# Softmax attention steps put in another order, bf16 decay rows and a new order of side work in a two-block transformer kernel on one Trainium2 core

## The chip, the cores and the metric

The kernel runs on one core of one Trainium2 chip. A core has four engines that compute: TensorE (PE, matrix products and transposes; its weight loads are shown apart as PEld), VectorE (DVE), ScalarE (ACT) and GpSimd (POOL), and SyncE (SP), whose queue issues nearly all weight loads here. Each engine works through its own queue in order, so an instruction that waits holds up all that stand behind it. The metric is the device time of one execution in microseconds (us); less is better.

## The reference

A 256 x 1024 activation `x` goes through a first block of two layers and a second block of two layers, all in fp32.

```python
# first block; layer 0 is even, layer 1 odd
y = even_mixer(rms(x))      # layer 0: 8 "fox" heads with a decay + 8 "nsa" heads (selected, window, compressed)
y = diff_mixer(rms(x))      # layer 1: 8 pairs of heads, a1 - lam * a2
x = x + rms(y); x = x + rms(memory_cross_attention(rms(x), rms(mem))); x = x + rms(swiglu(rms(x)))
# second block, each layer
x = x + 0.5 * swiglu(rms(x))
z = rms(x) @ w_in
mixed = sum(sigmoid(gate_i) * (y_i @ w_i))  # y: neighborhood attention, gated linear attention, latent attention
x = x + mixed @ w_out; x = x + 0.5 * swiglu(rms(x))
# fox attention
c = cumsum(log_sigmoid(f + bias)); s = q @ k.T / 8 + (c_q - c_k); p = softmax(masked s); o = p @ v
```

The softmax drops what is the same for all keys of a row, so of `c_q - c_k` only `-c_k` is added.

## The kernel before

All activations stay on chip. The 256 rows are two row tiles (`TT = 2`). A product with a weight matrix (`gemm_steps`) runs over *units* of weights of up to 2048 columns per partition: SP loads a unit into `raw`, ACT rounds it to `w_hi` (L449), DVE subtracts to get `w_lo` (L454, written over `raw`), and PE makes three products for each block of 128 weight rows (L593 to L595). There are six raw slots and three `w_hi` slots (`RAW_SLOTS`, `HI_SLOTS`). `part` emits the rounding and the subtraction, in one piece or in four.

Python generators are *fillers*: `fill(n)` emits n steps of work from them, a step of a weight product being six PE instructions (two blocks of rows, one row tile). A unit takes four steps. Outside attention `take` has every free unit prepared whole; within attention (`turn["gentle"]`) units are prepared in four pieces by `trickle`.

`attention(groups, ...)` handles two heads at a time (a group). In the order of the loop before: `trickle(2)`, `scores(i)` (PE: mask L805, q k L811), `turned(i-1)` (PE: transposes of the probabilities, L908), `maxed(i)` (DVE: row maximum, L842 or, with a bias, L835 and L838), `copied(i-1)` (transposes to `pT`, one half on ACT L921, the other on DVE L927), `exped(i)` (ACT, L867), `fill(a)`, `normed(i)` (DVE, L886 and L893), `summed(i-1)` (PE: value products L952, L958, L965), `fill(b)`. `probs` has one buffer. The plan gives (a, b) for each group.

There are these attention stages, in the profile's time: the even mixer (70 to 269 us; fox groups 0 to 3, then 12 nsa groups), memory attention (313 to 329 and 720 to 737 us, two groups, no filler), the odd mixer (578 to 672 us, 8 groups), neighborhood attention (1190 to 1274 and 1925 to 2007 us, 4 groups) and latent attention (1419 to 1450 and 2152 to 2184 us, 2 groups). The even mixer's fillers (`side`) are the nsa projections, then in this order the rotations of queries and keys with the gate's sigmoid (`sparse_keys`, L1343 to L1381, L1641, L1631), the memory keys and values of layer 0 (`memory_steps(0)`: transposes L532 with h_hi L568 and h_lo L584, then products), transposes, `compress` (L1680 to L1749) and `memory_steps(1)`. `rotate` shares its work between DVE and POOL and has one instruction for each row tile.

The decay of the fox heads is added by fp32 matmuls between the q k ones: a row of ones out of `ident` (8 rows) times `c_neg` (8 x 256), one for each head and row tile (L811, named `hT,const`).

## Time and profile before

| what | value |
|---|---|
| time, median of 3 runs | 2414.78 us (2404.65 to 2421.23) |
| the profiled execution, its time | 2420.43 us |
| its span, first to last instruction | 2418.8 us |
| PE busy | 2151.5 us (89%) |
| DVE busy | 1267.2 us (52%) |
| ACT busy | 1024.6 us (42%) |
| POOL busy | 165.1 us (7%) |
| TensorE clock granted, mean | 0.929 |

The span lies 1.6 us under the execution's own time, and that time 5.7 us over the median. The granted clock is the mean of two levels, 1.0 (2.4 GHz) and 0.5 (1.2 GHz).

### The profile page before, as it was taken

How to read it: one execution, taken by the hardware profiler on the slowest of the kernel's cores; microseconds unless marked ns; L12 is line 12 of the kernel's file. 1: busy time of each engine (PE TensorE's matmuls, PEld its weight loads, DVE VectorE, ACT ScalarE, POOL GpSimd, SP SyncE). 2: the span in 40 equal slices, each digit the busy share in tenths (PEclk: the TensorE clock that was granted, in tenths of full speed). 3: DMA queues.
4: the chain of work that ended last, by engine and by line, in shares of the span. 5: the costliest groups of instructions: out<-in, count | busy, mean ns of one | idle time of the engine just before them, and what ended most of it. 6: DMA issues, size and time to landing. Idle time of an engine off the chain costs nothing.

```text
span 2418.8 us, 26665 instructions
## 1 busy us (share of the span) xinstructions
PE 2151.5 (89%) x9943; PEld 1742.9 (72%) x9956; DVE 1267.2 (52%) x1767; ACT 1024.6 (42%) x1507; POOL 165.1 (7%) x200
## 2 busy tenths in 40 slices
PE   6968879999778999999978979999999978879998
PEld 5746568877566887887757757887887766757887
DVE  4435554555655445545455556545555546565454
ACT  4234444444444434444335435444444436345442
POOL 0010000000100000000202030000000202030000
PEclk8876779999888999999888989999999998989999
DMA  8212225554123554655533324655555433224553
GB/s 263 78 54 88 79 95 181 187 181 157 44 87 125 183 189 156 192 191 166 164 96 109 129 72 157 191 190 164 187 190 191 151 117 97 100 96 155 186 184 102
DMA packets 247751, 346.14 MB, mean 143 GB/s; under 512 B 28292, under 2 KB 177608, under 8 KB 247624
## 3 DMA queue, kind: packets, MB, share of 16 engines
q1 hardware_dynamic: 245816, 340.37, 44.0%
q10 hardware_dynamic: 1264, 2.79, 0.3%
q8 instruction: 81, 1.33, 0.2%
q0 software_dynamic: 544, 1.29, 0.2%
q14 instruction: 46, 0.38, 0.0%
HBM read 343.35 MB, written 2.33 MB: 143 GB/s over the span
## 4 chain that ended last, share of the span: by engine, by line
PE 76%; issue 8%; DVE 7%; ACT 4%; POOL 3%; ACTq 0%; DVEq 0%; POOLq 0%
PE bank L593 23%; PE bank L595 22%; PE bank L594 22%; DVE w_lo L454 2%; PE bank L811 2%; ACT w_hi L449 1%; PE bank L1088 1%; PE bank L958 1%; ACT h_hi L568 1%; PE bank L532 1%; DVE jobstat L842 1%; POOL o_buf L2080 1%; ACT probs L867 1%; DVE x L1249 1%; PE bank L952 1%
## 5 line engine op out<-in xcount | busy, mean ns | idle before, releaser
L454 DVE TENSOR_TENSOR w_lo<-raw,w_hi 128x2048 fp32r<-128x2048 f32 (+6 forms) x453 | 736.0, 1645 | 504.3 <-ACT w_hi L449 503.5
L593 PE MATMUL bank<-w_hi,h_hi 128*128 128x512 f32 (+4 forms) x1936 | 786.1, 406 | 135.4 <-DVE w_lo L454 85.6
L594 PE MATMUL bank<-w_lo,h_hi 128*128 128x512 f32 (+4 forms) x1936 | 767.1, 396 | 0.0
L595 PE MATMUL bank<-w_hi,h_lo 128*128 128x512 f32 (+4 forms) x1936 | 766.5, 396 | 0.0
L449 ACT CAST w_hi<-raw 128x2048 fp32r<-128x2048 f32 (+6 forms) x453 | 613.3, 1380 | 277.5 <-PE bank L595 265.7
L593 PEld LDWEIGHTS bank<-w_hi,h_hi 128*128 128x128 f32 x1936 | 383.7, 198 | 226.6 <-issue 69.9
L595 PEld LDWEIGHTS bank<-w_hi,h_lo 128*128 128x128 f32 x1936 | 382.4, 198 | 75.2
L594 PEld LDWEIGHTS bank<-w_lo,h_hi 128*128 128x128 f32 x1936 | 384.7, 199 | 68.6
L593 PE MATMUL bank<-w_hi,ff_hi 128*128 128x512 f32 x528 | 206.1, 390 | 0.0
L595 PE MATMUL bank<-w_hi,ff_lo 128*128 128x512 f32 x528 | 205.5, 389 | 0.0
L594 PE MATMUL bank<-w_lo,ff_hi 128*128 128x512 f32 x528 | 205.5, 389 | 0.0
L1067 ACT ACTIVATE ff_silu<-bank,rs 128x256 f32<-128x256 f32 x132 | 55.6, 472 | 200.9 <-PE bank L595 200.9
L1099 ACT CAST ff_hi<-bank 128x512 fp32r<-128x512 f32 x66 | 38.7, 587 | 235.8 <-PE bank L1088 235.8
L593 PEld LDWEIGHTS bank<-w_hi,ff_hi 128*128 128x128 f32 x528 | 99.1, 188 | 21.0 <-DVE ff_lo L1104 0.3
L1104 DVE TENSOR_TENSOR ff_lo<-bank,ff_hi 128x512 fp32r<-128x512 f32 x66 | 45.6, 691 | 131.0 <-ACT ff_hi L1099 131.0
L595 PEld LDWEIGHTS bank<-w_hi,ff_lo 128*128 128x128 f32 x528 | 99.1, 188 | 20.7
L594 PEld LDWEIGHTS bank<-w_lo,ff_hi 128*128 128x128 f32 x528 | 99.2, 188 | 20.3
L1076 DVE SCALAR_TENSOR_TENSOR ff_hid<-bank,rs,ff_silu 128x256 f32<-128x256 f32 x132 | 57.8, 479 | 86.3 <-ACT ff_silu L1067 86.3
L698 POOL TENSOR_TENSOR rs<-rs,const 128x2 f32<-128x2 f32 (+2 forms) x27 | 31.9, 1183 | 1041.4 <-DVE rs L693 1041.4
L568 ACT ACTIVATE h_hi<-bank,cols 128x256 fp32r<-128x256 f32 x128 | 49.9, 482 | 78.5 <-PE bank L532 48.7
L584 DVE SCALAR_TENSOR_TENSOR h_lo<-bank,cols,h_hi 128x256 fp32r<-128x256 f32 x128 | 52.3, 477 | 41.6 <-ACT h_hi L568 41.6
L811 PE MATMUL bank<-kT,qT 64*128 64x256 f32 (+2 forms) x320 | 61.1, 404 | 8.5 <-DVE kT L550 5.1
(248 smaller groups left out, 1665.0 us busy)
## 6 DMA issues: line engine op xcount, KB each, us to landing
raw<-in_ffn_w SPq DMA_DIRECT2D x176, 512.0 KB, 4.7
raw<-in_w_in SPq DMA_DIRECT2D x52, 1024.0 KB, 5.1
raw<-in_ffn_w SPq DMA_DIRECT2D x44, 1024.0 KB, 4.9
raw<-in_ffn_wg SPq DMA_DIRECT2D x44, 512.0 KB, 4.0
raw<-in_ffn_wu SPq DMA_DIRECT2D x44, 512.0 KB, 5.0
raw<-in_ffn_wd SPq DMA_DIRECT2D x22, 1024.0 KB, 4.8
raw<-in_od_w_in SPq DMA_DIRECT2D x12, 1024.0 KB, 5.1
raw<-in_w_out SPq DMA_DIRECT2D x8, 1024.0 KB, 5.1
```

The costliest lines, as they stand in the source:

```text
L449: act.copy(hi[:, cs], raw_[:, cs]).then_inc(*act_did.up())
L454: dve.tensor_tensor(lo_[:, cs], raw_[:, cs], hi[:, cs].bitcast(F32), ALU.subtract).then_inc(*dve_did.up())
L568: act.activation(dst(b0 + b, 1), ps[:, b:b + 1, :], ACT.Copy, scale=scale(b0 + b)).then_inc(*act_did.up())
L584: dve.scalar_tensor_tensor(dst_lo(b0 + b, 1), ps[:, b:b + 1, :], scale(b0 + b), dst(b0 + b, 1).bitcast(F32), ALU.mult, ALU.subtract).then_ ...
L593: pe.matmul(out, x_hi, u.hi[:, k, cols_], start=start, stop=False)
L594: pe.matmul(out, x_hi, u.lo[:, k, cols_], start=False, stop=False)
L595: return pe.matmul(out, x_lo, u.hi[:, k, cols_], start=False, stop=stop)
L811: mm = pe.matmul(view(i, j)[:, tt, 0:g["n"][tt]], l, r, start=(m == 0 and not masked), stop=(m == len(pairs) - 1), skip_group_check=True)
L1067: act.activation(ff_silu[:, c % 2, tt, :], bank.t[:, 0:FF_CHUNK], ACT.Silu, scale=r(tt)).then_inc(*act_did.up())
L1076: dve.scalar_tensor_tensor(ff_hid[:, c % 2, tt, :], bank.t[:, FF_CHUNK:2 * FF_CHUNK], r(tt), ff_silu[:, c % 2, tt, :], ALU.mult, ALU.mult) ...
L1099: act.copy(ff_hi[:, c % 2, :, :], ps).then_inc(*act_did.up())
L1104: dve.tensor_tensor(ff_lo[:, c % 2, :, :], ps, ff_hi[:, c % 2, :, :].bitcast(F32), ALU.subtract).then_inc(*dve_did.up())
```

## The change

- Attention loop: the order is now `turned(i-1)`, `copied(i-1)`, `fill(a)`, then `begin(i+1)` (`scores`, `maxed`, `exped` of the next group), `normed(i)`, `fill(b)`, `summed(i-1)`. `probs` has two buffers; `pT` lies in a spare half of `gain` or in `o_buf`. The 1/8 is put on q while it is copied out of its transposes, so that the separate scaling of the row maxima goes. `normed` takes the reciprocals of both heads in one instruction.
- Weights: in attention every filler step also calls `trickle` once; the subtraction of a piece is emitted after the rounding of the next; a unit is not begun until one step after its `w_hi` slot was last used (`LAG`).
- Fox decay: `-c` is split into three bf16 parts in 72 rows (`c3`), and one bf16 matmul of 512 columns for each head adds it.
- Even layer: the memory transposes and products are cut into four and put among the projections, before and between the rotations and `compress`; the order of the weight units follows.
- `rotate` is on DVE alone, both row tiles in one instruction.
- Plans: fox groups (5, 5) for (3, 3); neighborhood attention (4, 3) for (5, 5).

```diff
             while n > 0 and fillers:
                 if next(fillers[0], None) is None:
                     fillers.pop(0)
-                else:
-                    n -= 1
+                    continue
+                n -= 1
+                turn["steps"] += 1
+                if turn["gentle"]:
+                    trickle()
...
+            def low(cs, rounded):
+
+                @block.vector
+                def _(dve):
+                    dve.wait_ge(*rounded)
+                    dve.tensor_tensor(lo_[:, cs], raw_[:, cs], hi[:, cs].bitcast(F32), ALU.subtract).then_inc(
+                        *dve_did.up())
+                u.parted = dve_did.now()
+            behind = None
...
-                @block.vector
-                def _(dve):
-                    dve.wait_ge(*act_did.now())
-                    dve.tensor_tensor(lo_[:, cs], raw_[:, cs], hi[:, cs].bitcast(F32), ALU.subtract).then_inc(
-                        *dve_did.up())
-                u.parted = dve_did.now()
-                u.whole = p0 + n // pieces >= n
+                if behind is not None:
+                    low(*behind)
+                behind = cs, act_did.now()
+                if pieces > 1:
+                    yield True
+            low(*behind)
+            u.whole = True
+            if pieces == 1:
                 yield True
...
-            return n < len(of) and (n < slots or of[n - slots].used is not None)
+            if n >= len(of) or n < slots:
+                return n < len(of)
+            late = turn["gentle"] and of is split_units
+            return of[n - slots].used is not None and not (late and turn["steps"] - of[n - slots].at < turn["lag"])
...
             if turn["gentle"]:
                 load_more()
+                turn["lag"] = 0
                 while u.landed is None or (u.split and not u.whole):
                     trickle()
+                turn["lag"] = LAG
...
-                        if scale is None:
+                        if times is not None:
+                            dve.tensor_scalar(dst(b0, n), ps, times, None, ALU.mult).then_inc(*dve_did.up())
+                        elif scale is None:
                             dve.tensor_copy(dst(b0, n), ps).then_inc(*dve_did.up())
...
                                       start=True, stop=False, skip_group_check=True)
+                    if g.get("decay"):
+                        for j in range(2):
+                            l, r = g["decay"](j)
+                            pe.matmul(view(i, j), l, r, start=False, stop=False, skip_group_check=True)
...
             def exped(i):
@@ -859,37 +902,46 @@
                             act.wait_ge(*before.act)
                             act.wait_ge(*before.dve)
                             act.wait_ge(*before.pool)
-                        if i > 0:
-                            act.wait_ge(*st[i - 1]["turned"][j])
+                        if i > 1:
+                            act.wait_ge(*st[i - 2]["turned"][j])
                         for tt in range(TT):
                             n = g["n"][tt]
-                            p = probs[:, j, tt * T:tt * T + n]
+                            p = probs[:, i % 2, j, tt * T:tt * T + n]
...
+                @block.vector
+                def _(dve):
+                    dve.wait_ge(*s["exped"][1])
+                    if g.get("guard"):
+                        dve.tensor_scalar(sums, sums, 1e-30, None, ALU.max).then_inc(*dve_did.up())
+                        dve.wait_ge(*dve_did.now())
+                    dve.reciprocal(recip, sums).then_inc(*dve_did.up())
+                    dve.wait_ge(*dve_did.now())
+                    if g.get("mul"):
+                        at, by = g["mul"]
+                        r = js[:, 12 + at:16]
+                        dve.tensor_tensor(r.rearrange("p (j t) -> p j t", t=TT) if at == 0 else r,
+                                          r.rearrange("p (j t) -> p j t", t=TT) if at == 0 else r,
+                                          by, ALU.mult).then_inc(*dve_did.up())
+                        dve.wait_ge(*dve_did.now())
                 for j in range(2):
                     @block.vector
                     def _(dve):
...
+                            p = probs[:, i % 2, j, tt * T:tt * T + g["n"][tt]]
...
                 bank.drained = dve_did.now()
 
             turn["gentle"] = True
-            for i in range(len(groups) + 1):
-                a, b = plan(i) if plan else (0, 0)
-                trickle(2)
+            def begin(i):
+
                 if i < len(groups):
                     if groups[i].get("do"):
                         groups[i]["do"]()
                     scores(i)
-                if i >= 1:
-                    turned(i - 1)
-                if i < len(groups):
                     maxed(i)
                     if groups[i].get("scored"):
                         groups[i]["scored"]()
+                    exped(i)
+            begin(0)
+            for i in range(len(groups) + 1):
+                a, b = plan(i) if plan else (0, 0)
+                trickle()
                 if i >= 1:
+                    turned(i - 1)
                     copied(i - 1)
-                if i < len(groups):
-                    exped(i)
                 fill(a)
+                begin(i + 1)
                 if i < len(groups):
                     normed(i)
+                fill(b)
                 if i >= 1:
                     summed(i - 1)
-                fill(b)
             turn["gentle"] = False
             attended["o"] = marks()
...
+                    eng.tensor_tensor(t[dst], xx, table.unsqueeze(2).broadcast_to(shape), ALU.mult).then_inc(*sig.up())
 
...
+                products(dve, dve_did, ((0, x1, cos), (1, x2, sin), (2, x2, cos), (3, x1, sin)))
+                dve.wait_ge(*dve_did.now())
+                dve.tensor_tensor(x1, t[0], t[1], ALU.subtract).then_inc(*dve_did.up())
+                dve.tensor_tensor(x2, t[2], t[3], ALU.add).then_inc(*dve_did.up())
...
+                    dve.tensor_scalar(c3[:, :], decay, -1.0, None, ALU.mult).then_inc(*dve_did.up())
+                    dve.wait_ge(*dve_did.now())
+                    dve.scalar_tensor_tensor(c_rest[:, :], decay, -1.0, c3[:, :], ALU.mult,
+                                             ALU.subtract).then_inc(*dve_did.up())
+                    dve.wait_ge(*dve_did.now())
+                    for r0 in (32, 64):
+                        dve.tensor_copy(c3[r0:r0 + FOX_H, :], c_rest[r0:r0 + FOX_H, :]).then_inc(*dve_did.up())
+                    dve.wait_ge(*dve_did.now())
+                    dve.tensor_tensor(c3[64:PARTS_C, :], c_rest[64:PARTS_C, :], c3[64:PARTS_C, :],
+                                      ALU.subtract).then_inc(*dve_did.up())
...
             def side():
 
-                yield from gemm_steps(h_in, KD, NSA_CHUNKS, evac, ready)
+                HALF = KD // 2
+                for n, _ in enumerate(gemm_steps(h_in, KD, NSA_CHUNKS, evac, ready)):
+                    yield True
+                    if n == 19:
+                        yield from memory_turn(0, 0, 0)
+                yield from memory_turn(0, HALF, HALF)
+                sparse_queries()
+                yield from memory_multiply(0, 0, 0)
                 sparse_keys()
-                yield from memory_steps(0)
+                yield from memory_turn(1, 0, 0)
+                yield from memory_multiply(0, HALF, HALF)
                 groups = []
                 yield from to_T_steps(groups, 4, lambda b, tt: z[:, tt, EV["nq"] + b * P:EV["nq"] + (b + 1) * P],
-                                      lambda b, n: qT[:, 4 + b:4 + b + n, :], after=there["nq"])
+                                      lambda b, n: qT[:, 4 + b:4 + b + n, :], times=HD ** -0.5, after=there["nq"])
                 yield from to_T_steps(groups, 4, lambda b, tt: sq[:, tt, 512 + b * P:512 + (b + 1) * P],
                                       lambda b, n: kT[:, 4 + b:4 + b + n, :], after=there["sparse"])
                 there["turned"] = groups[-1]
-                yield from compress()
+                compressing = compress()
+                for _ in range(4):
+                    next(compressing)
+                    yield True
+                yield from memory_multiply(1, 0, 0)
+                yield from compressing
                 there["short"] = Marks(pe_did.now(), act_did.now(), there["compressed"], pool_did.now())
-                yield from memory_steps(1)
+                yield from memory_turn(1, HALF, 0)
+                yield from memory_multiply(1, HALF, 0)
             fillers.append(side())
...
             to_T(4, lambda b, tt: z[:, tt, EV["fk"] + b * P:EV["fk"] + (b + 1) * P],
@@ -1789,38 +1863,41 @@
             for hp in range(FOX_H // 2):
                 def qk(j, tt, hp=hp):
                     b, n = HD * j, (tt + 1) * P
-                    return [(qT[b:b + HD, hp, tt * P:(tt + 1) * P], kT[b:b + HD, hp, 0:n]),
-                            (ident[0:FOX_H, 2 * hp + j:2 * hp + j + 1].broadcast_to([FOX_H, P]), c_neg[:, 0:n])]
+                    return [(qT[b:b + HD, hp, tt * P:(tt + 1) * P], kT[b:b + HD, hp, 0:n])]
+
+                def decay(j, hp=hp):
+                    return (c_row[:, 2 * hp + j:2 * hp + j + 1].broadcast_to([PARTS_C, P]),
+                            c3[:, :].unsqueeze(1).broadcast_to([PARTS_C, TT, T]))
...
-            attention(groups, fox_turned, lambda i: (3, 3) if i < FOX_G else (1, 1))
+            attention(groups, flat(spare_gain(post_gain)), fox_turned, lambda i: (5, 5) if i < FOX_G else (1, 1))
+            gain_used[1 - post_gain[2]] = pe_did.now()
...
-            attention(groups, after, lambda i: (5, 5))
+            attention(groups, flat(o_buf[:, 0, :]), after, lambda i: (4, 3))
...
-            attention(groups, None, lambda i: (2, 2))
+            attention(groups, flat(gain[:, 0, :]), None, lambda i: (2, 2))
+            bias_free[:] = [attended["o"]] * 4
             start_branch(2, attended["o"])
```

What moved, at three places. First, DVE in neighborhood attention. `probs<-bank,gain` and `jobstat<-probs` are `maxed`, `RECIPROCAL` begins `normed`, `pT<-bank` (now `o_buf<-bank`) is `copied`, `w_lo` is a piece of a weight unit. Before:

```order
L835 SCALAR_TENSOR_TENSOR probs<-bank,gain 128x512
L838 TENSOR_REDUCE jobstat<-probs 128x2
L924 UNCONDITIONAL_BRANCH
L927 COPY pT<-bank 128x512
L451 UNCONDITIONAL_BRANCH
L454 TENSOR_TENSOR w_lo<-raw,w_hi 128x512
L451 UNCONDITIONAL_BRANCH
L454 TENSOR_TENSOR w_lo<-raw,w_hi 128x512
L879 UNCONDITIONAL_BRANCH
L886 RECIPROCAL jobstat<-jobstat 128x2
L893 TENSOR_SCALAR probs<-probs,jobstat 128x256 x2
L879 UNCONDITIONAL_BRANCH
```

Now:

```order
L875 SCALAR_TENSOR_TENSOR probs<-bank,gain 128x512
L878 TENSOR_REDUCE jobstat<-probs 128x2
L924 UNCONDITIONAL_BRANCH
L930 RECIPROCAL jobstat<-jobstat 128x4
L940 UNCONDITIONAL_BRANCH
L945 TENSOR_SCALAR probs<-probs,jobstat 128x256 x2
L940 UNCONDITIONAL_BRANCH
L945 TENSOR_SCALAR probs<-probs,jobstat 128x256 x2
L454 UNCONDITIONAL_BRANCH
L457 TENSOR_TENSOR w_lo<-raw,w_hi 128x512
L454 UNCONDITIONAL_BRANCH
L457 TENSOR_TENSOR w_lo<-raw,w_hi 128x512
```

The copy stands ahead of `maxed` now (above these rows), `maxed` belongs to the next group, and `normed` follows `maxed` directly; the `w_lo` pieces that stood in bunches between copy and `normed` come singly with the filler steps.

Second, ACT at the end of the nsa projections of the even layer. `stat<-z` is the gate's sigmoid, `h_hi` the memory's transposed rows, `w_hi` pieces of the memory's units. Before:

```order
L681 ACTIVATE z<-bank,rs 128x436
L1626 UNCONDITIONAL_BRANCH
L1631 ACT_TABLE_LOAD
L1631 ACTIVATE stat<-z 128x48
L557 UNCONDITIONAL_BRANCH
L568 ACTIVATE h_hi<-bank,cols 128x256 x2
L557 UNCONDITIONAL_BRANCH
L568 ACTIVATE h_hi<-bank,cols 128x256 x2
L444 UNCONDITIONAL_BRANCH
L449 CAST w_hi<-raw 128x512
L444 UNCONDITIONAL_BRANCH
L449 CAST w_hi<-raw 128x512
```

Now:

```order
L469 CAST w_hi<-raw 128x512
L464 UNCONDITIONAL_BRANCH
L469 CAST w_hi<-raw 128x512
L1034 UNCONDITIONAL_BRANCH
L1037 CAST oT_hi<-bank 128x256
L970 UNCONDITIONAL_BRANCH
L973 COPY gain<-bank 128x384
L1686 UNCONDITIONAL_BRANCH
L1691 ACT_TABLE_LOAD
L1691 ACTIVATE stat<-z 128x48
L584 UNCONDITIONAL_BRANCH
L597 ACTIVATE h_hi<-bank,cols 128x256 x2
```

The sigmoid, which waits for the rotations, stood ahead of the first memory rows and weights; now both halves of layer 0's rows and the pieces of its first weights stand ahead of it.

Third, PE in the last groups of the odd mixer, where no filler is left. `bank<-z,pT` (now `bank<-z,gain`) are value products, `bank<-const,probs` transposes, `bank<-kT,qT` scores. Before:

```order
L938 UNCONDITIONAL_BRANCH
L952 MATMUL bank<-z,pT 128x128 x6
L790 UNCONDITIONAL_BRANCH
L805 MATMUL bank<-bf_causal,bf_ident 128x512 x2
L811 MATMUL bank<-kT,qT 128x128 x2
L811 MATMUL bank<-kT,qT 128x256 x2
L903 UNCONDITIONAL_BRANCH
L908 MATMUL bank<-const,probs 128x128 x3
L903 UNCONDITIONAL_BRANCH
L908 MATMUL bank<-const,probs 128x128 x3
L938 UNCONDITIONAL_BRANCH
L952 MATMUL bank<-z,pT 128x128 x6
```

Now:

```order
L990 UNCONDITIONAL_BRANCH
L1004 MATMUL bank<-z,gain 128x128 x6
L955 UNCONDITIONAL_BRANCH
L960 MATMUL bank<-const,probs 128x128 x3
L955 UNCONDITIONAL_BRANCH
L960 MATMUL bank<-const,probs 128x128 x3
L826 UNCONDITIONAL_BRANCH
L841 MATMUL bank<-bf_causal,bf_ident 128x512 x2
L851 MATMUL bank<-kT,qT 128x128 x2
L851 MATMUL bank<-kT,qT 128x256 x2
L990 UNCONDITIONAL_BRANCH
L1004 MATMUL bank<-z,gain 128x128 x6
```

Before: value products of group i-1, scores of i+1, transposes of i. Now: value products of i-1, transposes of i, scores of i+2.

## Rows read from the trace of the kernel before

**Rows 1.** Busy time by engine, seven stretches: clock, DMA share, GB/s last
```profile
68.00:174.00 106.00, 81.57 (x335) 61.29 (x338) 38.10 (x99) 28.20 (x76) 7.23 (x30) 0.79 0.20 57
174.00:269.00 95.00, 79.02 (x437) 54.69 (x438) 58.91 (x205) 44.02 (x149) 0.00 (x0) 0.72 0.21 71
187.00:201.00 14.00, 13.82 (x64) 13.73 (x64) 1.36 (x3) 0.72 (x1) 0.00 (x0) 0.50 0.22 76
578.00:672.00 94.00, 73.05 (x387) 56.98 (x392) 52.99 (x145) 40.25 (x117) 6.48 (x13) 0.89 0.22 72
1186.00:1283.00 97.00, 73.52 (x322) 56.88 (x321) 49.12 (x96) 35.47 (x85) 8.18 (x11) 0.79 0.31 94
1415.00:1457.00 42.00, 38.33 (x173) 28.23 (x173) 20.06 (x43) 23.56 (x46) 1.88 (x2) 1.00 0.32 101
1921.00:2018.00 97.00, 72.36 (x328) 56.45 (x329) 50.77 (x96) 35.48 (x85) 8.80 (x12) 0.82 0.31 97
```

**Rows 2.** PE by line: 68-174, 578-672, 1186-1283, 1921-2018 us; L958 of the third
```profile
L593 PE MATMUL bank<-w_hi,h_hi 128*128 128x434 f32 (+2 forms) x60 | 27.9, 464 | 22.3 <-DVE w_lo L454 19.8 <-DVE jobstat L886 2.4
...
L593 PE MATMUL bank<-w_hi,h_hi 128*128 128x512 f32 x48 | 21.1, 440 | 8.9 <-DVE w_lo L454 4.7 <-DVE sq L1343 4.2
...
L593 PE MATMUL bank<-w_hi,h_hi 128*128 128x512 f32 (+1 forms) x70 | 32.1, 459 | 16.0 <-DVE w_lo L454 8.5 <-ACT w_hi L449 4.0 <-DVE jobstat L886 3.5
L958 PE MATMUL bank<-pT,z 128*64 128x256 f32 x32 | 6.1, 518 | 5.0 <-DVE jobstat L886 3.9 <-DVE pT L927 1.1
...
L593 PE MATMUL bank<-w_hi,h_hi 128*128 128x512 f32 (+1 forms) x72 | 31.8, 442 | 16.7 <-DVE w_lo L454 9.2 <-ACT w_hi L449 4.0 <-DVE jobstat L886 3.5
```

**Rows 3.** In order of time, ACT then PE, neighborhood attention, about 1243 us
```profile
1242.65 3.20 ACT L449 CAST w_hi<-raw 128x512 fp32r<-128x512 f32 x6
...
1244.72 0.77 PE L593 MATMUL bank<-w_hi,h_hi 128*128 128x512 f32 x1 [6.22 <-DVE w_lo L454]
```

**Rows 4.** In order of time, ACT then PE, even mixer, 144 to 151 us
```profile
144.24 1.28 ACT L1631 ACT_TABLE_LOAD   x1 [4.98 <-DVE z L1372]
...
145.68 1.55 ACT L568 ACTIVATE h_hi<-bank,cols 128x256 fp32r<-128x256 f32 x4
...
150.75 0.77 PE L593 MATMUL bank<-w_hi,h_hi 128*128 128x512 f32 x1 [11.28 <-DVE w_lo L454]
```

**Rows 5.** Line L811 alone, 68 to 174 us (four fox groups), PE and PEld
```profile
68.00:174.00 106.00, 19.74 (x64) 10.38 (x64) 0.79 0.20 57
```

**Rows 6.** PE in order of time, mask and scores, clock at 1.0, then 0.5
```profile
179.94 0.61 PE L805 MATMUL bank<-bf_causal,bf_ident 128*128 128x512 bf16 x2
180.47 0.93 PE L811 MATMUL bank<-kT,qT 64*128 64x128 f32 x8
...
254.90 1.03 PE L805 MATMUL bank<-bf_causal,bf_ident 128*128 128x512 bf16 x2
255.86 1.65 PE L811 MATMUL bank<-kT,qT 64*128 64x128 f32 x8
```

**Rows 7.** PE in order of time, odd mixer, groups without filler
```profile
643.26 0.88 PE L908 MATMUL bank<-const,probs 128*128 128x128 f32 x6
646.85 2.90 PE L952 MATMUL bank<-z,pT 128*128 128x128 f32 x12 [2.72 <-DVE jobstat L886]
...
651.02 0.88 PE L908 MATMUL bank<-const,probs 128*128 128x128 f32 x6
...
663.35 1.49 PE L908 MATMUL bank<-const,probs 128*128 128x128 f32 x6
```

**Rows 8.** DVE by line and shape, even mixer, 68 to 270 us
```profile
L842 DVE TENSOR_REDUCE jobstat<-bank 128x2 f32<-128x512 f32 x24 | 16.5, 687 | 27.0 <-PE bank L811 27.0
...
L893 DVE TENSOR_SCALAR probs<-probs,jobstat 128x256 f32<-128x256 f32 x24 | 8.4, 348 | 0.0
L893 DVE TENSOR_SCALAR probs<-probs,jobstat 128x128 f32<-128x128 f32 x24 | 6.9, 287 | 0.9
```

**Rows 9.** DVE in order of time, rotations of latent attention
```profile
1397.71 0.76 DVE L2523 TENSOR_TENSOR tmp<-tmp,vec 128x256 f32<-128x256 f32 x2
1398.67 1.55 DVE L1343 TENSOR_TENSOR sq<-z,const 128x128 f32<-128x128 f32 x4 [0.20 <-DVE tmp L2523]
1400.62 0.75 DVE L1372 TENSOR_TENSOR z<-sq 128x128 f32<-128x128 f32 x2 [0.40 <-POOL sq L1343]
...
1403.77 0.75 DVE L1372 TENSOR_TENSOR tmp<-gain 128x128 f32<-128x128 f32 x2 [0.40 <-POOL gain L1343]
```

192 lines of the change are left out of this document (96 added, 96 removed).

## The prediction

> **What bounds the kernel now.** I read the busy shares first: PE 89%, no other engine over 52%, so the end is set by PE's work, by its idle time (2418.8 - 2151.5 = 267 us) and by the level of its clock. Then I cut the span into stages and read PE busy and granted clock of each. The reader is to see that the feed-forward stages are not where time is lost: what the change touches are the stretches of [rows 1], the even mixer (68 to 269 us), the odd mixer (578 to 672), neighborhood attention (1186 to 1283 and 1921 to 2018) and latent attention (1415 to 1457; it comes twice, alike). In these PE idles 24.4, 16.0, 20.9, 23.5 and 24.6 us, and 3.7 us in latent attention. Third, PE by line gives what ended the idle time ahead of the weight products [rows 2]: 22.3, 8.9, 16.0 and 16.7 us, nearly all of it until DVE's `w_lo` or something DVE does ahead of `w_lo`. Last, the clock. Work done at level 0.5 takes twice as long, so a stretch loses about (1 - granted clock) x PE busy: 0.21 x 81.6 + 0.28 x 79.0 + 0.11 x 73.1 + 0.21 x 73.5 + 0.18 x 72.4 = 76 us for the five stretches of [rows 1] with waits.
>
> **The change part by part**, against the profiled execution (2420.4 us).
>
> *Decay rows.* The 64 score and decay matmuls of the four fox groups keep PE busy for 19.7 us [rows 5]. The same scores without decay take 0.93 us for a group, and two bf16 matmuls of 512 columns, here the mask's, 0.61 us; at the lower clock 1.65 and 1.03 us [rows 6]. So four groups will take 4 x (0.93 + 0.61) = 6.2 us, or 4 x 2.68 = 10.7 us at the lower level. The gain is 9 to 13.5 us of an engine that is busy around them; I take 11.5, since the clock is up in most of this stretch. The price of building `c3` is five small DVE instructions instead of one, once, beside the projection products; no row shows them at this size, a DVE row of 128x256 takes 0.35 us [rows 8], so 1.5 us of DVE, hidden by the products of the next chunk. If it were not, 1.5 us.
>
> *Weights in attention.* The rows of ACT and PE [rows 3] show the mechanism of the waits: ACT rounds six pieces in one run of 3.20 us, and only after the exponentials, because `take` emits them all when the unit is wanted; DVE follows; PE has stood still for 6.22 us. In the new order one piece goes out with each filler step, so a unit's four pieces go out while the unit before it is multiplied, and no exponential of the same group stands ahead of all four. The pool is 22.3 + 8.9 + 16.0 + 16.7 us [rows 2] less the 4.0 us in each neighborhood stage that end with ACT `w_hi` (they come after the last group, behind the norms, which nothing moves): 55.9 us. In the 22.3 us are the 11.28 us of [rows 4]: PE waits for the memory's `w_lo`, ACT had rounded rows and weights only after the sigmoid, and the sigmoid sat 4.98 us until DVE had ended the rotations. The new order puts two halves of memory rows and the first weights ahead of it, and the rotations lie beside products. I take 46 of the 55.9 us; bounds 35 and 56. What is late next are DVE's row maxima and normalisation, both of which now stand together in front of a piece.
>
> *Groups without filler.* The four last groups of the odd mixer have cycles of 7.76 us and (663.35 - 651.02) / 2 = 6.17 us from transposes to transposes [rows 7]; PE waits there for the copy to `pT`, which stands behind the next group's maxima on DVE. In the new order a cycle is transposes 0.88 [rows 7], mask and scores 1.47 (from 179.94 to 181.41 us) [rows 6], maxima 2 x 0.69 and normalisation of both heads 2 x (0.35 + 0.29) with about 0.2 for reciprocals [rows 8], and some 0.4 of hand-overs: 5.6 us, with the value products inside it. Three cycles give 3 us. In neighborhood attention the fillers ran out a group early (84 + 30 + 30 + 30 + 18 products); with (4, 3) they last to the last group, so of the 5.0 us in front of the value products [rows 2] about 1 stays: 4 us in each layer, 8 in both. For the twelve nsa groups and the two memory attentions the two orders come to nearly the same chain; I take 4 us together. Sum 15; bounds 22 gained and 8 lost, the loss if those chains are longer by 0.5 us in each of 16 groups.
>
> *Clock.* Where waits go, some of the 76 us returns. In 68 to 174 us waits make nearly all idle time, and I take 7 of its 17 us; odd mixer 2 of 8; neighborhood 6 of 28; the nsa tail, unchanged in kind, 3 of 22: 18 us. Bounds 8 and 35. Latent attention, with fillers in every group and no such waits, ran at 1.00 throughout [rows 1], which is the sight to expect in the filled groups. Against expecting more stands the stretch 187 to 201 us: PE busy for 13.82 of 14 us, and the clock at 0.50 throughout [rows 1]. The Trainium skill (TensorE: Matmul & The Clock Gate, Part 1) says that the default is the throttled state and that a busy PE releases the throttle. By that rule filled stages would give back all of the 76 us, and the sum would be 58 us lower; by the row they do not, as this busy stretch shows.
>
> *Rotations and ends.* A rotation of latent attention takes DVE from 1398.67 to 1404.5 us for q and k, 5.8 us on the path of a long PE wait, with four DVE instructions of 128x128 in 1.55 us beside POOL, and 128x256 ones at 0.34 us each without POOL [rows 9]. Twelve at 0.34 plus two waits are 4.5 us: 1.3 us gained in each layer, and for the ends of latent attention, where pieces are ready sooner, 0.7 each: 4 us in all, bounds 0 and 6. In the even and odd mixers the rotations are beside products and cost nothing; if the cover were gone they would cost the 6 us of DVE.
>
> *New waits.* Some 38 weight units run in the attention stages (6 projection, 4 memory, 6 odd, 16 neighborhood, 6 latent). I charge each 0.25 us of residual wait, an estimate from half a piece (1242.65: 3.20 / 6 = 0.53 us [rows 3]): 10 us, bounds 0 and 20. The scaling of q in its copy has the same sizes as the copy, the weights' new order the same bytes, and the gain loads wait for an attention that is over by then: nothing.
>
> Sum: -11.5 - 46 - 15 - 18 - 4 + 10 = -84.5, so 2336 us for the profiled execution. That one lay 5.7 us over the median, so the **forecast is 2330 us**. Taking all small ends together gives 9 + 35 - 8 + 8 + 0 - 20 = 24 us gained, all large ones 132; they will not all fall together.
>
> **The rivals.**
>
> *Weights stay late.* DVE is in order, and now maxima and normalisation of two groups stand together. If pieces are held behind them as they were behind the exponentials, most of the pool stays: -11.5 - 15 - 8 - 5 - 4 + 5 = -38.5, 2376 us. For it: two of the waits ended with DVE `jobstat` or `sq`, not with `w_lo`. Against it: the order shows pieces one by one among the rows. 0.20.
>
> *The clock comes all the way back.* Filled groups keep PE at level 1.0, as in latent attention [rows 1], and the nsa tail starts at it and stays there, so that all of the 76 us returns and not 18: -84.5 - 58 = -142.5, 2272 us. For it: the level fell in the five stretches where PE waited. Against it: the busy stretch at 0.50. 0.07. (This is what the rule of the Trainium skill's clock page, Part 1, would give.)
>
> *Longer chains where nothing fills.* Normalisation of group i waits behind the maxima of i+1, which wait for scores that are behind the transposes of i-1. With the clock at 0.5, transposes 1.5 and scores 2.7 us [rows 6, 7], the cycle is 7.2 us for the nsa groups. That is 20 us less gain, 2350 us. 0.10.
>
> *Slower.* The pieces' place on DVE is the mechanism. If each of the 38 units found its last piece behind one set of maxima and one normalisation, 1.38 + 1.5 = 2.9 us [rows 8], and a hand-over, 3.1 us, PE would wait 118 us where it now waits 56; with the clock and chain gains gone and only -11.5 and -4 left that is +46 us, 2461 us. It decides from (56 + 15.5) / 38 = 1.9 us of wait in each unit. Against it: products of a unit take 5 us on PE, and only one or two of a unit's four steps meet a group boundary. 0.04.
>
> *The change does not do what it says.* If fillers run out early in the groups where they matter, orders end alike. The order of PE shows them spread to the last neighborhood group, so 0.03, at 2415 us.
>
> **How the numbers follow.** Forecast 0.56, the others 0.20, 0.10, 0.07, 0.04, 0.03. The range 2292 to 2382 us takes in the first three and leaves out the full return of the clock, the slower case, the last, and a tail of the forecast's own bounds, together under 2 in 10. A measurement of this kernel tells about 1% from nothing. Faster by over 1% (under 2390.6 us): 0.56 + 0.10 + 0.07 + most of 0.20, about 0.90; within 1% 0.06; slower 0.04.
>
> **What the profile of the changed kernel would show.** Decay: the busy time of scores and decay in the fox stretch at 6 to 11 us against 19.7. Weights: idle time ahead of the L593 line's successor in the four stretches under 20 us in sum, no single wait over 3 us, and the 11.28 us gone. Chains: cycles of 5 to 6 us in the odd mixer's last groups. Clock: the first stretch at 0.85 to 0.9, neighborhood near 0.85, 174 to 269 us still near 0.75. Rotations: no POOL rows, 4.5 us in latent attention. The prediction is wrong if the `w_lo` waits are still there in bunches of 2 to 6 us, or if PE waits in front of transposes for the normalisation in groups that have filler.

## The result and the profile after

The changed kernel takes 2316.71 us (median of 4 runs, 2311.67 to 2318.63), the kernel before beside it 2416.7 us. The ratio is 0.959, 95% interval 0.9552 to 0.9629: faster. The forecast was 2330 us in a range of 2292 to 2382. The profiled execution took 2311.67 us, its span is 2309.7 us; by time it is 108.8 us under the profiled execution of before. PE is busy 2098.5 us, its mean clock 0.951.

The first reading cuts both kernels alike, at the first scores of an attention and at the first scores of the next: even mixer, odd mixer, neighborhood attention of each layer with what follows it. Columns: stretch, length, busy of PE, PEld, DVE, ACT and POOL, clock, DMA share, GB/s. Before:

```profile
70.90:313.70 242.80, 196.44 (x932) 146.56 (x938) 112.27 (x327) 86.86 (x251) 8.63 (x32) 0.77 0.22 69
579.00:720.00 141.00, 109.92 (x564) 88.22 (x567) 77.46 (x183) 58.73 (x152) 9.51 (x16) 0.88 0.24 76
1190.30:1419.10 228.80, 184.15 (x869) 147.17 (x869) 128.34 (x219) 93.26 (x158) 44.64 (x43) 0.86 0.32 102
1925.70:2152.50 226.80, 181.72 (x869) 145.54 (x869) 128.64 (x217) 93.23 (x158) 45.24 (x43) 0.86 0.32 103
```

The same four after:

```profile
71.00:272.00 201.00, 166.40 (x913) 128.50 (x912) 102.27 (x271) 86.17 (x250) 4.24 (x14) 0.84 0.26 83
535.60:657.60 122.00, 102.47 (x567) 82.15 (x567) 73.35 (x159) 58.05 (x152) 4.67 (x4) 0.94 0.27 88
1122.40:1328.80 206.40, 177.91 (x869) 143.77 (x869) 128.09 (x214) 93.53 (x159) 38.76 (x31) 0.88 0.37 118
1836.30:2042.20 205.90, 178.00 (x868) 143.60 (x869) 126.81 (x213) 94.02 (x160) 38.82 (x31) 0.89 0.37 118
```

The four stages are 104.1 us shorter (839.4 less 735.3). Length less busy gives PE's idle time: 167.2 us before, 110.5 after, 56.7 less. (1 - clock) x busy gives what the clock costs: 109.6 before, 73.7 after, 35.9 less. What remains of busy time, the work counted at full clock, is 11.6 us less. The clock has two digits here; added up over slices of 1 us the last two figures are 37.4 and 10.0. All other stages together give 5 us.

To see where the clock's share comes back, each of the four is cut once more close behind its last group of heads, at the same place of PE's work in both kernels. The attention parts before:

```profile
70.90:268.90 198.00, 159.56 (x762) 115.38 (x768) 94.93 (x302) 71.63 (x223) 7.23 (x30) 0.75 0.20 62
579.00:672.90 93.90, 72.75 (x387) 56.87 (x391) 53.63 (x146) 40.03 (x117) 6.48 (x13) 0.89 0.21 68
1190.30:1284.40 94.10, 73.17 (x312) 56.37 (x313) 44.82 (x90) 32.68 (x79) 8.18 (x11) 0.78 0.30 90
1925.70:2018.00 92.30, 70.39 (x312) 54.66 (x313) 46.07 (x90) 32.66 (x79) 8.76 (x11) 0.82 0.30 92
```

And after:

```profile
71.00:226.90 155.90, 129.25 (x743) 97.09 (x742) 84.93 (x246) 71.17 (x223) 2.85 (x12) 0.84 0.25 79
535.60:611.80 76.20, 66.88 (x391) 51.84 (x390) 51.94 (x126) 40.83 (x120) 1.64 (x1) 0.98 0.25 84
1122.40:1194.60 72.20, 65.96 (x313) 52.39 (x314) 44.20 (x86) 33.70 (x81) 8.03 (x11) 0.86 0.42 132
1836.30:1909.00 72.70, 66.46 (x312) 52.60 (x313) 43.71 (x86) 33.65 (x81) 8.10 (x11) 0.86 0.41 129
```

By the same product the clock costs 76.7 us in the attention parts before and 40.5 after. Behind them it costs 32.6 us before and 31.8 after, hardly less. So all of the 36 us comes back within the attention parts: 19 in the even mixer, 7 in the odd one, 10 in the two neighborhood attentions.

The lines that answer to [rows 2]: the first product line of PE in the fox groups, the odd mixer and both neighborhood attentions.

```profile
L622 PE MATMUL bank<-w_hi,h_hi 128*128 128x434 f32 (+2 forms) x68 | 26.2, 385 | 0.0
L622 PE MATMUL bank<-w_hi,h_hi 128*128 128x512 f32 x48 | 19.9, 414 | 1.5 <-ACT z L711 1.5
L622 PE MATMUL bank<-w_hi,h_hi 128*128 128x512 f32 (+1 forms) x72 | 30.5, 423 | 4.0 <-ACT w_hi L469 4.0
L622 PE MATMUL bank<-w_hi,h_hi 128*128 128x512 f32 (+1 forms) x72 | 30.7, 426 | 4.0 <-ACT w_hi L469 4.0
```

63.9 us of waits are 9.5, and 8.0 of these are the ones that the prediction had left out as unmoved. But two waits of another form have come, in the even mixer. PE, then ACT, each in order of time:

```profile
130.46 1.01 PE L841 MATMUL bank<-bf_causal,bf_ident 128*128 128x512 bf16 x2 [5.62 <-DVE w_lo L457]
152.70 13.85 PE L1766 MATMUL bank<-hT,raw 128*128 128x45 f32 x64 [5.80 <-DVE gain L979]
```

```profile
127.07 1.14 ACT L469 CAST w_hi<-raw 128x512 fp32r<-128x512 f32 x2 [4.39 <-DMA raw<-in_ca_wv]
...
150.03 0.62 ACT L469 CAST w_hi<-raw 128x512 fp32r<-128x512 f32 x1 [4.16 <-DMA raw<-in_ev_w_out]
150.56 0.37 ACT L1037 CAST oT_hi<-bank 128x256 fp32r<-128x256 f32 x1
...
151.34 0.48 ACT L973 COPY gain<-bank 128x384 f32<-128x384 f32 x1
```

Each time ACT has been handed a piece of a unit whose load was issued but had not landed. ACT stands for 4.39 and 4.16 us, and what stands behind on ACT are copies that DVE and PE need. The name that PE's wait carries is only the last link.

The decay: scores and decay matmuls of the fox groups by line, 71 to 129 us (one matmul record is missing).

```profile
L851 PE MATMUL bank<-kT,qT 64*128 64x128 f32 (+1 forms) x32 | 3.7, 350 | 0.0
L846 PE MATMUL bank<-c,c_row 72*128 72x512 bf16 x7 | 2.2, 379 | 0.0
```

5.9 us, some 6.2 with the missing matmul, stand against the 19.74 of [rows 5]. The last groups of the odd mixer, PE in order of time, against [rows 7]:

```profile
592.75 0.98 PE L960 MATMUL bank<-const,probs 128*128 128x128 f32 x6 [1.00 <-ACT probs L910]
...
597.73 0.97 PE L960 MATMUL bank<-const,probs 128*128 128x128 f32 x6 [1.19 <-ACT probs L910]
...
603.16 0.98 PE L960 MATMUL bank<-const,probs 128*128 128x128 f32 x6 [1.62 <-ACT probs L910]
```

A cycle is 5.0 and 5.4 us. The rotation of latent attention on DVE, against [rows 9]:

```profile
1308.93 1.43 DVE L1400 TENSOR_TENSOR sq<-z,const 128x256 f32<-128x256 f32 x4 [0.20 <-DVE tmp L2602]
...
1313.16 0.42 DVE L1411 TENSOR_TENSOR tmp<-gain 128x256 f32<-128x256 f32 x1
```

From 1308.93 to 1313.58 it takes 4.65 us. The clock, against [rows 1]: the fox groups, the nsa tail, both neighborhood attentions, latent attention.

```profile
68.00:174.00 106.00, 89.77 (x500) 72.77 (x500) 54.73 (x137) 48.80 (x131) 2.85 (x12) 0.86 0.32 99
162.00:235.00 73.00, 58.08 (x322) 39.40 (x322) 38.11 (x130) 29.18 (x112) 0.00 (x0) 0.75 0.18 63
...
1118.00:1212.00 94.00, 84.25 (x395) 67.09 (x396) 55.15 (x98) 47.72 (x98) 8.03 (x11) 0.87 0.39 124
1324.00:1366.00 42.00, 37.55 (x168) 27.20 (x168) 20.76 (x44) 23.39 (x46) 1.55 (x1) 1.00 0.30 101
1832.00:1925.00 93.00, 83.40 (x389) 66.04 (x388) 52.52 (x96) 48.24 (x99) 8.10 (x11) 0.87 0.40 125
```

### The profile page after: what moved, and what is told of

It is laid out like the page before. It is cut to its first block, busy times and chain, and to the rows that moved or that the text cites. A ratio compares the mean times of both kernels' runs of the same rounds, so it can differ in the third digit from the quotient of the medians.

```text
span 2309.7 us, 26412 instructions
## 1 busy us (share of the span) xinstructions
PE 2098.5 (91%) x9932; PEld 1709.9 (74%) x9932; DVE 1249.0 (54%) x1669; ACT 1022.5 (44%) x1501; POOL 139.7 (6%) x134
## 4 chain that ended last, share of the span: by engine, by line
PE 79%; issue 8%; DVE 6%; ACT 3%; POOL 2%; DMA 1%; DVEq 0%; ACTq 0%; SPq 0%; POOLq 0%
PE bank L622 24%; PE bank L624 23%; PE bank L623 23%; PE bank L960 1%; PE bank L1141 1%; PE bank L851 1%; POOL o_buf L2159 1%; PE bank L557 1%; ACT w_hi L469 1%; PE bank L1010 1%; ACT h_hi L597 1%; DMA raw<-in_ev_w_in 1%; DVE w_lo L457 1%; DVE x L1306 1%; DVE jobstat L884 1%
## 5 line engine op out<-in xcount | busy, mean ns | idle before, releaser
L457 DVE TENSOR_TENSOR w_lo<-raw,w_hi 128x2048 fp32r<-128x2048 f32 (+5 forms) x447 | 739.0, 1665 | 466.2 <-ACT w_hi L469 465.6
L622 PE MATMUL bank<-w_hi,h_hi 128*128 128x512 f32 (+4 forms) x1936 | 771.8, 399 | 75.1 <-DVE w_lo L457 39.9
L624 PE MATMUL bank<-w_hi,h_lo 128*128 128x512 f32 (+4 forms) x1936 | 757.2, 391 | 0.0
L623 PE MATMUL bank<-w_lo,h_hi 128*128 128x512 f32 (+4 forms) x1936 | 756.5, 391 | 0.0
L469 ACT CAST w_hi<-raw 128x2048 fp32r<-128x2048 f32 (+5 forms) x447 | 616.5, 1396 | 313.8 <-PE bank L624 295.3
L622 PEld LDWEIGHTS bank<-w_hi,h_hi 128*128 128x128 f32 x1936 | 376.6, 195 | 161.0 <-issue 52.0
L624 PEld LDWEIGHTS bank<-w_hi,h_lo 128*128 128x128 f32 x1936 | 375.8, 194 | 72.6
L623 PEld LDWEIGHTS bank<-w_lo,h_hi 128*128 128x128 f32 x1936 | 377.1, 195 | 67.0
L1120 ACT ACTIVATE ff_silu<-bank,rs 128x256 f32<-128x256 f32 x132 | 55.6, 473 | 201.0 <-PE bank L624 201.0
L910 ACT ACTIVATE probs<-bank,jobstat 128x256 f32<-128x256 f32 (+2 forms) x128 | 51.5, 416 | 70.4 <-DVE jobstat L884 55.8
```

The source lines that it names most:

```text
L457: dve.tensor_tensor(lo_[:, cs], raw_[:, cs], hi[:, cs].bitcast(F32), ALU.subtract).then_inc(*dve_did.up())
L469: act.copy(hi[:, cs], raw_[:, cs]).then_inc(*act_did.up())
L622: pe.matmul(out, x_hi, u.hi[:, k, cols_], start=start, stop=False)
L623: pe.matmul(out, x_hi, u.lo[:, k, cols_], start=False, stop=False)
L624: return pe.matmul(out, x_lo, u.hi[:, k, cols_], start=False, stop=stop)
L910: act.activation(p, p if g.get("bias") else view(i, j)[:, tt, 0:n], ACT.Exp, bias=js[:, 4 + 2 * j + tt:5 + 2 * j + tt], scale=1.0 if g.get ...
```

## The experiments

"Before" ran beside each on the same chip; "even" is the even mixer of the profiled execution, cut as above.

| run | median us | ratio | 95% interval | even us |
|---|---|---|---|---|
| single pieces undone | 2412.62 | 0.9982 | 0.9967 to 0.9998 | 228.2 |
| loop order undone | 2302.44 | 0.9526 | 0.9505 to 0.9548 | 191.9 |
| single pieces alone, on the kernel before | 2356.58 | 0.9734 | 0.9701 to 0.9767 | 239.6 |
| side work undone | 2325.10 | 0.9615 | 0.9591 to 0.9640 | 215.6 |
| changed kernel again | 2322.91 | 0.9600 | 0.9575 to 0.9626 | 203.6 |
| fp32 decay | 2339.28 | 0.9681 | 0.9653 to 0.9708 | 219.3 |
| plans undone | 2306.73 | 0.9551 | 0.9527 to 0.9575 | 194.4 |
| idle PE filled | 2310.98 | 0.9560 | 0.9536 to 0.9583 | 201.0 |
| pieces wait for the load | 2296.52 | 0.9495 | 0.9464 to 0.9526 | 184.5 |
| loop and plans undone | 2316.16 | 0.9561 | 0.9530 to 0.9592 | 193.8 |
| loop and plans undone, load rule, PE filled | 2285.62 | 0.9438 | 0.9408 to 0.9469 | 183.9 |
| loop, plans and single pieces undone | 2401.96 | 0.9920 | 0.9892 to 0.9948 | 214.8 |

**Single pieces undone.**

```diff
-                if turn["gentle"]:
-                    trickle()
...
-LAG = 1
+LAG = 0
...
-                trickle()
+                trickle(2)
```

> The changed kernel, but with the weights emitted as in the kernel before: no piece with a filler step, two at the head of each group, the rest when the unit is wanted, and no lag. Theory (the single pieces are what removes the waits): the waits in front of weight products come back, 35 to 56 us, and with them 5 to 15 us of clock, so 2360 to 2385 us. Rival (scores a group ahead remove them, since DVE and ACT are then free when a unit is wanted): most of the gain stays, 2317 to 2335 us.

The subtraction, too, follows its rounding directly again, so three things are undone together: the piece with each step, the late subtraction and the lag. No run takes them apart. It is 96 us slower than the changed kernel: nearly the whole gain is gone, more than theory said, and the rival falls. The first product line of PE shows where (over the whole program; the changed kernel has 75.1 us of waits in the same line, 39.9 of them until `w_lo`):

```profile
L614 PE MATMUL bank<-w_hi,h_hi 128*128 128x512 f32 (+4 forms) x1936 | 784.3, 405 | 132.7 <-DVE w_lo L455 107.4 <-ACT h_hi L589 11.6 <-ACT sq L735 5.6
```

**Loop order undone**, the loop as in the kernel before, with `trickle()` at its head.

> The changed kernel, but with the loop of attention in the order of before (scores, transposes of the last group, maxima, copies, exponentials, filler, normalisation, value products, filler), single pieces kept. Theory: only the groups without filler lose, 3 us in the odd mixer, 8 in neighborhood attention, some 4 elsewhere and a little clock: 2325 to 2340 us. Rival (the order of the loop is the main term, the pieces follow from it): 2350 us or more.

Both fall: it is faster than the changed kernel, by 14 us of the medians, and the intervals don't meet. The odd mixer (122.2 us against 122.0) and both neighborhood attentions (206.9 and 206.8 against 206.4 and 205.9) are as long as with the new order, and the groups without filler at the end of the odd mixer have cycles of 5.4, 5.2 and 4.8 us; the whole difference is in the even mixer.

**Single pieces alone.** The diff of the first experiment the other way round, in the kernel before.

> The kernel before with one part of the change alone: one piece of a weight unit with each filler step, the subtraction a piece later, the lag of one step. Order of the loop, side work, decay, plans and rotations are those of before. Theory: it gets most of the 46 us by itself, less the 11 us that are the order of side work, and some clock: 2370 to 2385 us. Rival (pieces are held behind exponentials and maxima whatever step they go out with): 2400 to 2420 us.

More than theory: 58 us of the 98 by this part alone, and the odd mixer has come down from 141.0 to 123.7 us, neighborhood attention from 228.8 and 226.8 to 208.2 and 212.9. In the even mixer it gives only 3 us: there ACT stands at pieces whose loads have not landed for 14.15, 4.95 and 12.54 us, and behind the first two of these PE waits 8.54 and 6.31 us.

**Side work undone.**

```diff
+                sparse_queries()
+                sparse_keys()
+                for k0 in (0, HALF):
+                    yield from memory_turn(0, k0, 0)
+                    yield from memory_multiply(0, k0, 0)
```

> The changed kernel, but with the even layer's side work and its weight units in the order of before (projections, both rotations and the sigmoid, then memory rows and products in turn, compress, memory of layer 1). Theory: the 11.28 us wait behind the sigmoid comes back, with 2 to 6 us for the clock after it: 2328 to 2336 us. Rival (the new order only moves the wait to another place, since the changed kernel waits 5.6 and 5.8 us before and after compress): 2312 to 2321 us.

The wait behind the sigmoid [rows 4] is back as one of 7.1 us, and two others in the even mixer are 8.5 and 6.1 us. By the order of ACT the 8.5 us are again a load (columns as above):

```profile
129.32 0.62 ACT L468 CAST w_hi<-raw 128x512 fp32r<-128x512 f32 x1 [7.40 <-DMA raw<-in_ca_wv]
```

The even mixer is 12 to 15 us longer in the profile (215.6 against 203.6 and 201.0), but the medians are only 2 to 8 us apart and the intervals overlap. The term has the right sign and place; its size these runs don't tell. The median, 2325.10 us, lies between the two forecasts.

**Four on one chip.** The first is the changed kernel again.

> The changed kernel once more, for runs on the same chip as the three kernels with it. Both theories: 2311 to 2320 us.

Its median, 2322.91 us, lies 3 us above the stated range (five runs, 2312.45 to 2323.68). The same kernel thus gave two medians 6 us apart, and differences of that size between sets are not read here.

The fp32 decay:

```diff
-                    return [(qT[b:b + HD, hp, tt * P:(tt + 1) * P], kT[b:b + HD, hp, 0:n])]
+                    return [(qT[b:b + HD, hp, tt * P:(tt + 1) * P], kT[b:b + HD, hp, 0:n]),
+                            (ident[0:FOX_H, 2 * hp + j:2 * hp + j + 1].broadcast_to([FOX_H, P]), c_rest[0:FOX_H, 0:n])]
```

> The changed kernel, but with the decay of the fox heads added by the fp32 matmuls of before (8 rows, one for each head and row tile between the q k ones), and one DVE instruction to make their rows. Theory: 10 to 13 us slower than the changed kernel, 2326 to 2330 us, all of it busy time of PE in the fox groups. Rival (part of the matmuls' time lies in waits that the changed kernel has there anyway, 5.6 and 5.8 us): 2317 to 2323 us.

16.4 us slower, more than either had. The busy time of the two kinds of matmul, by line over 72 to 135 us:

```profile
L851 PE MATMUL bank<-c_rest,const 8*128 8x128 f32 (+1 forms) x32 | 10.7, 418 | 0.0
L851 PE MATMUL bank<-kT,qT 64*128 64x128 f32 (+1 forms) x32 | 10.3, 404 | 0.0
```

The q k ones alone go from 3.7 us to 10.3 when the others stand between them. The two lines overlap in time: counted once, all 64 take 19.03 us, against 6.2 in the changed kernel, 13 more. PE's busy time is 19.0 us more in all (2121.7 against 2102.7), its idle time 1.5 us less; so nothing of it lies in waits, and the rival falls.

Part of the 16.4 us is clock. The second group shows the price at full clock, from 86.61 to 90.83 us:

```profile
86.61 0.48 PE L851 MATMUL bank<-kT,qT 64*128 64x128 f32 x2
...
90.14 0.69 PE L851 MATMUL bank<-c_rest,const 8*128 8x256 f32 x2
```

That is 4.22 us. The same group of the changed kernel takes 1.45 us (78.45 to 79.90), so the four groups cost 11.1 us more. The stretch from the first mask matmul to where the products with `early` begin holds the same other work in both runs, and PE is busy in nearly all of it; first the changed kernel again, then the fp32 decay:

```profile
70.30:125.50 55.20, 55.00 (x303) 45.21 (x303) 34.73 (x86) 29.55 (x80) 2.84 (x12) 0.97 0.34 100
72.20:143.20 71.00, 70.95 (x326) 54.60 (x326) 35.07 (x86) 29.65 (x80) 2.85 (x12) 0.90 0.27 77
```

It is 15.8 us longer. The clock costs 7.1 us of it against 1.7, 5.4 more, and the other 10.4 us fit the 11.1.

The plans, `(3, 3)` for `(5, 5)` in the fox groups and `(5, 5)` for `(4, 3)` in neighborhood attention:

> The changed kernel, but with the filler plans of before: (3, 3) for the fox groups, (5, 5) in neighborhood attention. Theory: neighborhood attention runs out of filler a group early, 4 us in each layer, and the fox groups lose nothing: 2322 to 2328 us. Rival (the plans decide nothing now that pieces go singly): 2312 to 2320 us.

Both fall: 16.2 us faster, and each of its five executions is faster than each of the changed kernel's. Neighborhood attention keeps its length (206.4 and 205.7 us), so the plan alone gives nothing there; in the even mixer the old plan is 9 us better. ACT, PE and ACT in the even mixer, where the changed kernel waits 5.80 us:

```profile
146.40 0.48 ACT L973 COPY gain<-bank 128x384 f32<-128x384 f32 x1 [0.30 <-PE bank L960]
149.44 8.61 PE L1766 MATMUL bank<-hT,raw 128*128 128x45 f32 x64
154.84 1.66 ACT L469 CAST w_hi<-raw 128x512 fp32r<-128x512 f32 x3 [7.96 <-DMA raw<-in_ev_w_out]
```

ACT still stands at the same load, for 7.96 us, but the copy that PE needs now goes ahead of the piece. PE's wait is gone, and its 64 matmuls take 8.61 us where they took 13.85 at the lower clock. With the loop's order undone it is the same: ACT stands 11.10 us at this load with the copy ahead of it, PE does not wait, and the 64 take 9.23 us. The other wait, of 5.62 us, stays in both (6.50 and 5.13 us).

PE filled while it waits:

```diff
+                    if i == 0 and turn["attentions"] > 0:
+                        for _ in range(WARM_FIRST):
+                            pe.matmul(view(i, 0), bf_ident[:, :], CAUSAL, start=True, stop=True,
...
+                        if j == 0 and not fillers:
+                            for _ in range(WARM_EACH):
+                                pe.matmul(bank.t[:, :].rearrange("p (t k) -> p t k", t=TT), bf_ident[:, :], CAUSAL,
```

> The changed kernel with idle PE filled by work that changes nothing: 6 more mask matmuls of 512 columns ahead of the first scores of each attention but the first, while PE waits there, and 4 ahead of the transposes of each group for which no filler is left, into a bank that is overwritten. Theory (the clock falls after waits, and a busy PE keeps it at 1.0): the loss by the clock shrinks from 82 us to 50 to 65, and since the added matmuls fit into the waits only in part, the time is 2295 to 2312 us. Rival (the level there does not come from the waits): the loss stays within 5 us of 82, and the time is 2317 to 2335 us.

The theory holds in kind: by (1 - clock) x busy over the span, the loss goes from 109 us (0.052 x 2102.7) to 89 (0.042 x 2109.3), though busy time rose by 6.6 us; 11.9 us faster. By the count of the expectation, added up over slices of 1 us so that only busy time at the lower level enters, it is 86 and 69 us, where 50 to 65 were forecast. The two intervals of the ratio just overlap, so the 11.9 us are less certain than the clock. Not all comes back: the 64 matmuls of `compress` stay at 0.50 and take 13.85 us here too.

**The load and the rest.** The rule on loads:

```diff
             while free(split_units, turn["parted"], HI_SLOTS) and split_units[turn["parted"]].landed is not None:
+                if pieces > 1 and turn["lag"] and turn["steps"] - split_units[turn["parted"]].issued < LAND:
+                    return
```

> The changed kernel, with one rule more: within attention no piece of a weight unit is emitted until four filler steps after the unit's load was issued. Theory (the waits of 5.6 and 5.8 us in the even mixer are ACT standing at a piece whose load has not landed, with the copies for PE behind it): both waits go, with 0 to 4 us of clock, 2305 to 2313 us. Rival (the pieces are then missed at the weight products, so the wait only moves): 2317 to 2328 us.

Better than theory: the gain over the kernel before grows from 4.1 to 5.0 per cent (ratio 0.9590 to 0.9495) by one rule. The waits of 5.62 and 5.80 us are gone, and the even mixer is at 184.5 us:

```profile
72.70:257.20 184.50, 161.34 (x913) 124.29 (x912) 102.36 (x271) 86.36 (x250) 4.24 (x14) 0.87 0.29 90
```

Idle time there is 23.2 us against 34.6, and the clock costs 21.0 us against 26.6. ACT stands once more at a load, for 3.01 us, with no wait of PE over 2 us behind it. By the profiled executions the rule is worth 15 or 21 us (2296.35 against 2311.67 and 2317.42), and the even mixer alone is 16 or 19 us shorter; by the medians it is 20 or 26.

> The changed kernel with the loop's order of before and the plans of before; kept are single pieces, decay rows, side work and rotations. Theory (the two undone parts cost by the same ACT waits for a load in the even mixer): no more is gained than by the better one alone, 2300 to 2308 us. Rival (they add up, 12 and 16 us): 2288 to 2296 us.

Both fall. The two do not add up: 2316.16 us is 9 to 14 us slower than either alone and no faster than the changed kernel. In its neighborhood attentions, with both the old order and the old plan, stand the 4 and 6 us that neither cost alone (210.4 and 211.7 us); the even mixer is as short as with either (193.8).

> The changed kernel with the loop's order and the plans of before, the rule on loads of the first run of this set and the mask matmuls that fill PE's waits. Theory (loads and clock are separate costs): 2280 to 2296 us. Rival (what is left of the even mixer is one chain, and filling only lengthens it): 2298 to 2310 us.

As the theory had it: 2285.62 us, faster than both kernels, and clock 0.967. Against the rule on loads alone that is 0.0057 of ratio, or 14 us; 11 by the medians. It differs from that run in the order and the plans too, so what the filled waits give of it is not shown.

> The changed kernel without the single pieces, and with the loop's order and the plans of before too: decay rows, side work and rotations are the change that is left. Theory (they give what they gave when undone, 16 + 8 us and about 3): 2385 to 2397 us, and the new loop and plans then cost 15 to 28 us where weights come in bunches. Rival (without single pieces nothing of them is left, the waits for weights take it back): 2405 to 2417 us.

Between the two. Decay rows, side work and rotations are worth 20 us by themselves here (0.9920), not the 27 of the single terms. The run with loop and plans undone differs from it in the single pieces alone, and is 86 us faster: that is what the pieces are worth there. And against the first experiment, which has the new order and plans, it is 11 us faster by the medians, 15 by the ratios: where weights come in bunches the new order and plans cost something too, at the low end of the 15 to 28.

## Why the prediction held, and where it did not

The range and the direction held. Term by term, with the four stages above as measure:

- **Decay rows, -11.5.** At full clock the term is 11.1 us by the fp32 run, and work at full clock fell by 10 to 12 us in the four stages: it was sized rightly. What the new matmuls take was right too ("6.2"), and the old ones took 19.03 us in the fp32 run against the 19.74 read. Undone it cost 16.4 us: 5.4 of them are the fox stretch at a clock of 0.90 and not 0.97, which the term left out. The bf16 rows were not put into the kernel before alone.
- **Weights in attention, -46, new waits +10, groups without filler -15, ends -4.** Together 55 us less idle time forecast, 56.7 measured. The sum is right, its parts are not, and that they made up for each other is luck. The waits in front of products fell by 54.4 us (63.9 to 9.5), so nearly the whole pool went, not 46 of 55.9. In front of the products the only waits over 3 us are the two of 4.0 that had been set aside. But the 10 us of new waits were priced as 38 small ones and are two, of 5.6 and 5.8 us, one of them under the name `w_lo` and of the size that the prediction called a sign of being wrong. Their cause is not the residue of half a piece that the step priced. It is a piece of a unit that has not landed, with the copies behind it on ACT. No term of the prediction asked when the load behind a piece lands; the run with the rule on loads shows that one should have, and that its lack costs 15 to 26 us.
- **Groups without filler.** Cycles of 5.0 and 5.4 us match "5.6". But the credit to the order of the loop was wrong: with the old order and single pieces the odd mixer is 122.2 us too, with cycles of 5.4, 5.2 and 4.8 us, and PE's idle time there is some 11.5 us less than before either way; with the pieces alone, in the kernel before, it is 123.7. What shortens the stage are the pieces. In neighborhood attention the 8 us are there only when order and plan are both undone (4 and 6 us); either of them is enough.
- **Clock, -18.** This is the mis-sized term: 35.9 us in the four stages. In the stretches that the prediction named it read well (0.86, 0.75, 0.87, 0.87 against "0.85 to 0.9", "near 0.75", "near 0.85"). The pool was right as well: 76.7 us in the attention parts, of which 36 came back and not 18. The share taken of it was too small everywhere: 10 forecast and 19 measured in the even mixer, 2 and 7 in the odd one, 6 and 10 in neighborhood attention. The shares were chosen and came from no row, and why twice as much came back no run takes apart. The products behind the attentions run at the lower level too, at a cost of 32.6 us that no term counted, but it did not move. That more of PE busy means more of the higher level is supported by the run with PE filled; that waits are the only thing that lowers it is refuted (see the last section), and so is that it comes back whole.
- **Rotations.** 4.65 us in latent attention against "4.5". POOL's work in them is gone.
- **What is not in the sum.** The new order of the loop and the new fox plan each cost the even mixer some 10 us, but not one on top of the other: either undone, or both, makes it 7 to 12 us shorter. Both do it by where a piece stands that meets its load: with either undone the copy for PE goes ahead of the piece, the wait of 5.80 us is gone, and the 64 matmuls behind it take 4.6 to 5.2 us less. That is 10 to 11 us. With order and plans kept, the rule on loads takes 16 to 19 us off. So the changed kernel gained by the pieces, the decay rows and the rest, and gave some back by the new order of the loop and the plan. Of the order nothing is left as a gain but this: with the old plans the old order costs neighborhood attention 4 and 6 us.

The rival "weights stay late" fell at the product lines. "Longer chains" was left without a trace that decides it; its own terms add up to 7.5 us for a cycle and not 7.2. "The clock comes all the way back" fell too, though the time came out on its side of the forecast. "Slower" had its mechanism in the right place, pieces on in-order engines, but with the wrong partner: it was ACT at a load, not DVE at a maximum.

The profiled execution is 24 us under the 2336 of the sum (the median 13 under the forecast). 18 of the 24 are the clock term, 5 lie in the stages that no term named, and under 2 in the idle time, where the parts were off by more than that.

## What to carry to other kernels

Spread preparatory work (here roundings and subtractions of weights) one piece per step of the engine that it feeds: here that, with the late subtraction and the lag, was worth 58 us by itself and 86 to 96 in the changed kernel, and where no load was late the order of the steps around it then made no difference. Then ask of every piece that is emitted early not only whether its slot is free but whether its data will be there when an in-order engine reaches it, because all behind it pays. And give the clock a term of its own, cut by stage: in the attention parts here 36 us came back with 54 us of removed waits, and the products behind them kept their 32 us of cost.
